# HGRN2 head loop: the key products move from GpSimd to VectorE, and GpSimd keeps only the weight split

## What is computed

```python
q = silu(hq) * HG_DK ** -0.5
f_f = lb[0] + (1 - lb[0]) * sigmoid(hff)        # f_b the same from hfb
of, sf = gla_scan(q, 1 - f_f, iv, log(f_f), s0_hg[:, 0])
ob, sb = gla_scan(flip(q), flip(1 - f_b), flip(iv), flip(log(f_b)), s0_hg[:, 1])
o_hg = head_rms(of + flip(ob)) * hg_norm_w * silu(hog)
# gla_scan, per chunk, with b = cumsum(log f):
a = einsum('bthk,bshk,btshk->bhts', qc, kc, exp(b[:, :, None] - b[:, None, :]))   # causal
o = einsum('bhts,bshv->bthv', a, vc) + einsum('bthk,bhkv->bthv', qc * exp(b), s)
s = exp(b_last)[..., None] * s + einsum('bshk,bshv->bhkv', kc * exp(b_last - b), vc)
```

## Time and profile before

| | us |
|---|---|
| median of 3 runs | 2137.21 |
| lowest and highest | 2135.84, 2141.61 |
| span of the profiled execution (first to last instruction) | 2134.4 |
| TensorE matmul busy in the span | 1954.5 (92%) |
| VectorE busy | 1106.8 (52%) |
| GpSimd busy | 1131.8 (53%) |
| ScalarE busy | 464.6 (22%) |

### The profile page before, as it was taken

How to read it: one execution, slowest core, us unless ns; L and a number is a source line. 1 busy time by engine, 2 the same in 40 slices (tenths; PEclk the granted TensorE clock), 3 DMA queues, 4 the chain that set the end, 5 groups by cost and what they waited for, 6 DMA issues and landing times.

```text
span 2134.4 us, 34113 instructions
## 1 busy us (share of the span) xinstructions
PE 1954.5 (92%) x13036; PEld 1919.0 (90%) x13036; DVE 1106.8 (52%) x1458; ACT 464.6 (22%) x671; POOL 1131.8 (53%) x644
## 2 busy tenths in 40 slices
PE   5998999998888888888888999799998999999997
PEld 4998999998777877888878999799997999999997
DVE  8776676577478889888794222600033321222123
ACT  2301010011334443444433222300012210000011
POOL 4454665557455566555664333245556455455555
PEclk8999999999899999999999999999999999999999
DMA  7342343343211111111112121022212122122222
GB/s 272 126 158 99 109 157 145 122 157 112 85 33 45 54 42 42 34 44 54 42 33 86 60 77 51 25 79 79 79 63 76 60 79 72 67 79 79 79 67 91
DMA packets 52485, 176.71 MB, mean 83 GB/s; under 512 B 6848, under 2 KB 9664, under 8 KB 52032
## 3 DMA queue, kind: packets, MB, share of 16 engines
q1 hardware_dynamic: 47952, 170.11, 22.7%
q10 hardware_dynamic: 4464, 5.64, 0.8%
HBM read 171.00 MB, written 4.72 MB: 82 GB/s over the span
## 4 chain that ended last, share of the span: by engine, by line
PE 68%; DVE 14%; issue 10%; POOL 3%; ACT 2%; DMA 1%; DVEq 1%; SPq 0%; ACTq 0%; POOLq 0%
PE acc L323 62%; DVE ada_prod L413 3%; DVE hg_qlev L786 1%; DVE hg_eb L767 1%; DVE hg_eb L768 1%; DVE hg_ef L762 1%; PE mix L933 1%; POOL hg_klev L804 1%; DVE hg_qlev L787 1%; PE mix L1223 1%; PE mix L953 1%; PE mix L966 1%; DMA ada_raw<-ada_dram 1%; POOL hg_klev L808 1%; POOL w_hi L311 1%
## 5 line engine op out<-in xcount | busy, mean ns | idle before, releaser
L311 POOL TENSOR_SCALAR w_hi<-raw 128x1024 fp32r<-128x1024 f32 x240 | 289.9, 1208 | 807.3 <-PE acc L323 706.9
L323 PE MATMUL acc<-h_hi,w_hi 128*128 128x320 f32 x2816 | 665.2, 318 | 33.2 <-DVE h_lo L517 31.8
L323 PE MATMUL acc<-h_lo,w_hi 128*128 128x320 f32 x2816 | 648.6, 312 | 0.0
L323 PE MATMUL acc<-h_hi,w_lo 128*128 128x320 f32 x2816 | 647.4, 311 | 0.0
L313 POOL TENSOR_TENSOR w_lo<-raw,w_hi 128x1024 fp32r<-128x1024 f32 x240 | 615.6, 2565 | 20.0
L323 PEld LDWEIGHTS acc<-h_hi,w_hi 128*128 128x128 f32 x2816 | 476.0, 191 | 39.6 <-issue 34.3
L323 PEld LDWEIGHTS acc<-h_lo,w_hi 128*128 128x128 f32 x2816 | 478.8, 191 | 0.0
L323 PEld LDWEIGHTS acc<-h_hi,w_lo 128*128 128x128 f32 x2816 | 476.6, 190 | 0.0
L413 DVE CUSTOM_DVE_ANT_0 ada_prod<-ada_raw,c_row 128x1024 f32<-128x1024 f32 x130 | 232.5, 1824 | 4.9 <-DMA ada_raw<-ada_dram 2.1
L528 DVE SCALAR_TENSOR_TENSOR x<-acc,mod,x 128x128 f32 x168 | 63.2, 433 | 238.6 <-PE acc L323 238.0
L323 PE MATMUL acc<-u_hi,w_hi 128*128 128x320 f32 x704 | 163.1, 313 | 13.3 <-DVE x L528 13.2
(11 more groups left out here) (215 smaller groups left out, 2028.4 us busy)
## 6 DMA issues: line engine op xcount, KB each, us to landing
raw<-w_dram SPq DMA_DIRECT2D x240, 512.0 KB, 3.7
ada_raw<-ada_dram SPq DMA_DIRECT2D x65, 512.0 KB, 5.2
ada_pe<-ada_pe_dram SPq DMA_DIRECT2D x7, 512.0 KB, 9.5
x<-x_dram SPq DMA_DIRECT2D x2, 1280.0 KB, 9.7
y_dram<-x SPq DMA_DIRECT2D x8, 320.0 KB, 2.4
c_row<-in_c_dram SPq DMA_DIRECT2D x1, 1024.0 KB, 4.5
hg_sin<-s_hg_dram ACTq DMA_DIRECT2D x8, 128.0 KB, 2.0
out_hg_dram<-hg_sfin ACTq DMA_DIRECT2D x8, 128.0 KB, 1.7
```

Source lines behind the costliest of these rows:

```text
L311: pool.tensor_scalar(w_hi[:, slot, :], raw[:, slot, :], 1.0, 1.0, ALU.mult, ALU.mult).then_inc(hi_done, 1)
L323: last = pe.matmul(acc[g][:, b, 0:HT], w[:, s, k * P:(k + 1) * P], tile[:, b * HT:(b + 1) * HT], start=(k == 0 and n == 0), stop=(k == k_t ...
```

## The change

`hg_keys` is called from VectorE's program, right behind `hg_operands` of the same level. Its waits on `hg_exp` and `hg_lev` fall away, since `hg_operands` has just waited for both. GpSimd's HGRN2 program is now a plain loop over splits.

```diff
-        def hg_keys(pool, m, u):
+        def hg_keys(dve, m, u):
...
             if u == 0:
-                pool.wait_ge(hg_key, 2 * m + 2)
-            pool.wait_ge(hg_exp, N_ARG * m + u + 1)
-            if u >= 1:
-                pool.wait_ge(hg_lev, (LEVELS + 1) * m + u)
+                dve.wait_ge(hg_key, 2 * m + 2)
...
-                pool.tensor_tensor(out[:, :, first], blocks(k_f[:], u)[:, :, first], fb[:, :, first], ALU.mult)
-                pool.tensor_tensor(out[:, :, second], blocks(k_b[:], u)[:, :, second], bb[:, :, second],
-                                   ALU.mult).then_inc(hg_kk, 1)
+                dve.tensor_tensor(out[:, :, first], blocks(k_f[:], u)[:, :, first], fb[:, :, first], ALU.mult)
+                dve.tensor_tensor(out[:, :, second], blocks(k_b[:], u)[:, :, second], bb[:, :, second],
+                                  ALU.mult).then_inc(hg_kk, 1)
             else:
                 k, e = (k_f, e_f) if u == LEVELS else (k_b, e_b)
-                pool.tensor_tensor(k_lev[:, s, :], k[:], e[:, s, :], ALU.mult).then_inc(hg_kk, 1)
+                dve.tensor_tensor(k_lev[:, s, :], k[:], e[:, s, :], ALU.mult).then_inc(hg_kk, 1)

         def split_hg(pool):

-            for p in range(5):
-                split_slab(pool, "hg", p, 0)
-            split_slab(pool, "hg", 0, 1)
-            with pool.Fori(1, HG_HEADS - 1) as h:
-                split_and_keys(pool, "hg", h, "hg", 0, h + 1)
...
+            with pool.Fori(0, HG_HEADS) as h:
+                for p in range(5):
+                    split_slab(pool, "hg", p, h)
+            for p in range(6):
+                split_slab(pool, "ret", p, 0)
...
                 hg_operands(dve, m, u)
+                hg_keys(dve, m, u)
                 hg_score_read(dve, m, u)
...
-            hg_operands(dve, m, LEVELS)
-            hg_operands(dve, m, LEVELS + 1)
+            for u in (LEVELS, LEVELS + 1):
+                hg_operands(dve, m, u)
+                hg_keys(dve, m, u)
```

## The result

| | before | after |
|---|---|---|
| median of six runs (us) | 2137.19 (2132.56 to 2141.61) | 2147.17 (2144.77 to 2148.14) |
| span of the profiled execution (us) | 2134.4 | 2145.3 |
| VectorE busy (us) | 1106.8 | 1117.1 |
| GpSimd busy (us) | 1131.8 | 971.3 |

After stands to before as 1.0043, 95% interval 1.0033 to 1.0054. The forecast was 13 us faster, 2124.2 with a range of 2104 to 2144. The kernel became 10 us slower and lies 3 us above the range.

What follows compares the result with a forecast made beforehand. VectorE was taken to bound levels and turn. Levels 59 us less, turn 42 more and the first head's start 4 more gave -13, from 2137.21 to 2124.2 us, range 2104 to 2144.

Steps and rivals of the forecast that it cites:

- turn, with Q' and O' in it: States, next head's start, scans and first arguments: 19.8 us before, two more slab splits add 6.0 on VectorE.
- V' beside the levels: Split of one slab, staying in the levels: costs VectorE 2.7 us a head, between 1.9 and 2.96.
- VectorE's idle time in the levels: VectorE's waits for TensorE within the levels: 1.6 us a head before, 0.8 after.
- F': Split of a next-head slab, beside the last long key products: costs VectorE 1.7 us, midway between 3.4 and nothing.
- levels: First query product to last key product of a head: 35.1 us after, against a mean of 42.5 before.
- wait for the state products: VectorE's idle stretch after the last key product: stays at 4.4 us a head, transposes and state products being unchanged.
- swap of the key products alone: Key products moved from GpSimd to VectorE in the levels: 7.1 us added, about 7.5 regained, only the 1.4 tail won.
- The new places of the splits: Freed from queueing behind key products, two slab splits move from levels to turn, costing 6.0 us; a third stays.
- The fourth rival: Three splits, in turn and levels, hold VectorE for whole instructions, 3.45 us each: 13 us more, time 2137; chance 0.08.
- the first: Rival: splits stand aside for dense VectorE rows in levels and turn: about 2097 in full, halfway 2110; chance 0.19.
- The second rival: The split beside the last long key products costs its full 3.4 us in each head: time 2138; chance 0.19.
- third rival: TensorE's clock falls after its wait at unit 0 and TensorE sets the levels' pace: 21 us more, 2145; chance 0.14.

Runs made afterwards that it cites:

- the run without keys: Key products left out, on the kernel before: 2043.18 us; on the changed kernel with every split held at its old place: 2042.65 us.
- the run with the filler: Changed kernel with 28 more TensorE transposes, results unread, between the transposes of the two key products: 2135.01 us, 0.9993 of before.

## Why the prediction was wrong, by its own steps

| us per head | forecast | measured |
|---|---|---|
| turn, with Q' and O' in it | 25.8 | 25.68 |
| V' beside the levels | 2.7 | 1.9 |
| VectorE's idle time in the levels | 0.8 | 1.4 |
| F' | 1.7 | 3.0 |
| levels | 35.1 | 36.45 |
| wait for the state products | 4.4 | 5.97 |
| swap of the key products alone | 1.4 | 3.9 |

**What bounds the kernel: right.** VectorE bounds levels and turn, in every experiment: it idles at most 2.8 us in the levels of any head.

**The new places of the splits: right.** Q' follows B' into the scans, O' comes behind it, V' stays in the levels (from 8.8 us on, where 6 was taken). The two that moved cost the turn 5.9, as against 6.0. The fourth rival (3.45 each) is out by this, and so is the first, that splits stand aside: V' alone did so, for its first instruction, which the 1.9 to 2.96 of the prediction had room for.

**"F' ... I take the middle, 1.7": wrong.** The start of F' was worked out nearly right: 784.64 lies in the second of the four long products, where the third was forecast, so that the first instruction of the split stretches the third and its second the fourth, as was forecast. Then a middle was taken between 3.4 and nothing. But the place is set by TensorE's pace, and in this kernel it was the same in each head, so the answer was all or nothing in all of them: the median of the last key products is 2.956 us, the longest 2.958. It paid 3.0 in seven heads. In the eighth, which is the last, the next split belongs to another phase, came earlier (1114.61) and cost 2.3 there. The second rival said just this and had 0.19.

**"The wait of 4.4 stays, since the transposes and state products are as they were": wrong.** They are the same instructions, but not at the same clock. The stretched key product makes TensorE wait 3.8 us, its clock falls, and the chain from the last key product to the state gets 1.6 longer. The prediction knew of such a step: its third rival took the low stretch behind a wait from the earlier trace rows and looked for it behind unit 0. There it came too (2.50 for unit 0 after 6.82), and the read of the scores at 754.88 did not wait for it. It was not looked for behind F', where nothing covers it. A stall was priced on the engine that it stretches, and not on the engine that waits for that one. These two steps, 1.3 and 1.6 us in seven heads, are 20 us and bring the forecast from 2124 to 2144.5: they are why there was no gain.

**Idle time: mis-sized.** 0.57, 0.57 and 0.24 us before three reads of scores, 1.4, where 0.8 was taken. The runs show where it comes from. Over six heads (676 to 1076 us) these waits are 8.7 us in the change and 10.5 with F' alone held, where Q' and O' are out of the levels; they are 3.1 with Q' and O' held back into the levels and 1.5 with all splits held. So the levels get ahead of TensorE once Q' and O' have left them. V' costs about 1 us more in the last two runs than in the first two, so it has a part in this.

Per head these are +1.3, +1.6, +0.6 and -0.8 for V', together +2.7, 19 us in seven periods. From the first query product of the first head to that of the last (618.03 to 1094.17) the seven periods took 476.1 us, for 7 x 65.3 = 457.1 of the forecast: 19.0 more. The time up to that first query product missed by 2: it grew by 6.2 (611.86 to 618.03), for a forecast of 4 (1 to 6), and 0.7 of this already stood at VectorE's first instruction of the loop (600.84 for 600.12). The splits of Q' and O' met no scan there, but what stands ahead of the scans, for example L837:

```profile
603.22 2.69 DVE L837 TENSOR_SCALAR hg_kf<-hg_kf,lb_rest 128x640 f32<-128x640 f32 x1
605.83 0.54 DVE L837 TENSOR_SCALAR hg_kb<-hg_kb,lb_rest 128x640 f32<-128x640 f32 x1
```

The last head and what follows it missed by 2.5, of it 2.0 more idle time. The sum is 24, from 13 less to 11 more in the span of the profiled executions (10 more on the medians).

**"Taken alone the swap wins only the tail": wrong, though the sum did not use it.** The sum went from the old levels, as measured, to new ones built of dense rows, and so had the gain of the swap in it unseen. The sentence took GpSimd's key products at 7.5 + 1.4 by a remainder, from which VectorE's waits for TensorE had been taken out. Most of them belonged to the key products. Had the swap been priced by the run without keys, its 3.9 a head would have stood against the 4.6 of F', and the question would have been how to keep F' where it was.

**What decided the sign**: the swap gains 30 us, and the free splits give back 40. Of these, 36 are F' and what hangs on it. The other 4 are what Q', O' and V' at their new places cost on balance: about 1.5 us a head more idle time in the levels (10.5 against 1.5 us in six heads), against 0.6 less for the splits themselves (7.8 for three, where three at their old places cost 8.4).

## What to carry to other kernels

When work leaves an in-order engine, the work that stays on it moves up. Find where each remaining instruction lands in a steady period, and take the landing as nearly the same in every turn: an unknown that is all or nothing is carried through the sum as its two ends, each with its chance, not as a middle. Follow a stretched instruction through to the engine that waits for it, since its wait (3.8 us here) may cost TensorE its clock as well. And keep a wait that held other work out of the way: here one semaphore wait made the difference between 10 us slower and 26 us faster.

## What the runs showed of the hardware that was not expected

- GpSimd does not always get its turn at VectorE's next instruction. At 762.09 a `w_hi` of 1.05 us took 2.39: three products of VectorE started after it, and it ended about 1 us after VectorE went idle at 763.57. At 784.64, beside 640 column products, it took 1.52 and VectorE's next one was held up. In one head of the run with the filler the same instruction took 3.01 and held up none of the last long products. The Trainium skill, "SBUF — State Buffer", "SBUF: two separate sides", gives the shared ports to whichever engine starts first for one whole instruction; the rows show a waiting GpSimd instruction passed over several times. What decides it was not found.
- Beside dense work of VectorE a split costs about the same wherever it stands: two more among the scans of a turn cost 5.9 us, three among the products of a level 8.8. It is free in VectorE's idle wait, and 1.0 cheaper where its first instruction meets a short pause (V', 1.9 for 2.9).
- ScalarE is a cheap place for such a conversion: 1024 columns of `w_hi` take it 1.05 us, in the rows shown no instruction of VectorE is stretched beside it, and each one taken off GpSimd is 0.8 us off VectorE's path.
- TensorE's clock fell behind a pause of 3.81 us in a chain of dependent work, not in it: the granted clock was 1.00 for the first 0.7 us of work behind the pause and 0.50 from 791 to 794 us. Transposes whose results nobody reads, put into the pause, kept it at 1.00.
